# Gate and value projections by seven products of half-size blocks in place of eight, with the products sent to the down projection through DRAM

## The chip, the cores and the metric

One core of a Trainium2 chip (trn2). The metric is the device time of one execution in microseconds. The kernel before takes 2325.32 us, the median of 3 runs (2323.78 to 2327.04).

## The reference, cut to what matters

One layer of a hybrid model on 1024 prompt tokens and 8 x 4 sample tokens: a projection, a gated linear recurrence and sparse attention, an output projection, and then a feed-forward block with a short convolution over time. Only that last block is touched:

```python
def conv_ffn(h, conv_past, w_gate, w_val, conv_w, conv_b, w_down):
    u = h @ w_gate
    u_ext = jnp.concatenate([conv_past.astype(u.dtype), u], axis=1)
    c = conv_b + u_ext[:, 0:T] * conv_w[0]
    for j in range(1, CONV_W):
        c = c + u_ext[:, j:j + T] * conv_w[j]
    y = (jax.nn.gelu(c) * (h @ w_val)) @ w_down
    return y, u_ext[:, T:]
```

h is [1056, 1024] (prompt and samples together), w_gate and w_val are [1024, 2816], w_down is [2816, 1024], all float32. The last two rows of u of every sequence are outputs too.

## The kernel before, in words

Every large product is made with split operands: a value x is kept as a high part H (x rounded to fp32r by ScalarE) and a low part L = x - H (by VectorE), and a product is HH + HL + LH, three matmuls. The sizes: P = 128, TOK = 1056 tokens, KD = 8 blocks of 128 along the model axis, NF = 22 tiles of 128 along the feed-forward axis, PW = 352 = TOK / 3.

`project_out` (line 951) makes x1 = x + o @ w_out by tiles of 128 tokens (9 tiles, the last has 32) and the normalized, transposed h. For each tile VectorE adds (L1135), ScalarE squares (L1068), VectorE scales (L1101), TensorE transposes (L1170), and `keep_hT` (L1103) writes the high part of h (L1107) and, in four operations, the low part (L1111) for each of two halves of the model axis. They stay in SBUF for the next stage, as hH and hL. SyncE loads the first weights of the next stage at L1017.

`feed_forward` (line 1206) has two parts.

Projections. For each tile f of 128 features, first the gate (a = 0), then the value (a = 1): three parts of 352 tokens, 8 blocks along the model axis, 3 matmuls each, in the loop around L1585, which runs over f in hardware (Fori). Each tile's weights are [128, 8, 128]: SyncE loads them (L1299), ScalarE makes the high part (L1354), VectorE the low part (L1457). The gate's result is copied by ScalarE to U (L1361 to L1364), convolved over time by VectorE into C (L1470 to L1475, prompt and samples apart), put through gelu by ScalarE (L1369), and multiplied by VectorE with the value's result straight out of PSUM (L1490) into aT, which stays in SBUF, three tensors of [128, 22, 352] for the three parts of the tokens. GpSimd has nothing to do in this part.

Down projection. 12 units (3 parts of tokens x 4 quarters of the output), each of 11 pieces of w_down ([128, 2, 256], 256 KB; SyncE L1307, a ring of 4), each piece 12 matmuls (L1619). ScalarE and VectorE split each piece (L1379, L1497) and each pair of tiles of aT (L1390, L1502). Between them TensorE turns the results of the unit before (L1594), ScalarE copies (L1396), VectorE adds x1 (L1511) and normalizes at the end of each part (L1531). GpSimd issues the loads of x1 and the stores of y (L1324, L1330).

The order of the work on every engine is the order in which it is written; semaphores join the engines:

```python
            for i in range(2, PIECES):
                n, g = i // NGR, i % NGR
                high_w(i)
```

Of the kernel before, what the change touches and what calls it, by code (L numbers as in the profile page):

```python
# [5 lines left out]
F32 = mybir.dt.float32  # L6
# [944 lines left out]
def project_out(nc, io, keep, scratch, consts_sb):  # L951

    ident, hH, hL = consts_sb["ident"], keep["hH"], keep["hL"]
    with ExitStack() as ctx:
# [8 lines left out]
        oH, oL = keep["wH"], keep["wL"]  # L963
        sq = sb("sq", [P, D])
# [12 lines left out]
        hH_ready, low_added = sem("hH_ready"), sem("low_added")  # L977
        scaled = sem("scaled")
        rs = keep["hg_ss"]
# [17 lines left out]
        def _(sp):  # L997
# [18 lines left out]
            for a, w in enumerate(("w_gate", "w_val")):  # L1016
                sp.dma_start(keep["raw"][:, a], io[w][0].rearrange("(k p) n -> p k n", p=P)[:, :, 0:P]).then_inc(soft[f"p6_wu_in{a}"], 16)  # L1017
# [22 lines left out]
        def _(act):  # L1040
# [20 lines left out]
            for t in range(NT):  # L1061
# [6 lines left out]
                nc.scalar.activation(sq[0:r, :], x1[0:r, t % 2, :], ACT.Square, accum_out=ss[0:r, t:t + 1]).then_inc(ss_ready, 1)  # L1068
                act.wait_ge(ms_ready, t + 1)
                nc.scalar.activation(rt[0:r, t:t + 1], ss[0:r, t:t + 1], ACT.Sqrt).then_inc(root_ready, 1)  # L1070
                if t == 3:
                    act.wait_ge(conv_turned, 1)
                    turned = to[1][:].rearrange("p k c -> p (k c)")
                    nc.scalar.copy(keep["cw"][:].rearrange("p f j -> p (f j)"), turned[:, 0:20 * NF]).then_inc(conv_kept, 1)

        @block.vector
        def _(dve):
# [25 lines left out]
            def keep_hT(t):  # L1103
                r = rows_of(t)
                for h in range(2):
                    dve.wait_ge(hT_ready, 2 * t + h + 1)
                    nc.vector.tensor_tensor(hH[:, 4 * h:4 * h + 4, t * P:t * P + r], th[h][:, :, 0:r],  # L1107
                                            g2[:, 4 * h:4 * h + 4].unsqueeze(2).to_broadcast([P, 4, r]), ALU.mult).then_inc(hH_ready, 1)
                    dve.wait_ge(hH_ready, 2 * t + h + 1)
                    for k in range(4):  # L1110
                        last = nc.vector.scalar_tensor_tensor(hL[:, 4 * h + k, t * P:t * P + r], th[h][:, k, 0:r],  # L1111
                                                              g2[:, 4 * h + k:4 * h + k + 1],
                                                              hH[:, 4 * h + k, t * P:t * P + r].bitcast(F32), ALU.mult, ALU.subtract)
                    last.then_inc(hT_kept, 1)

            lows = Steps(dve, low_added)
# [5 lines left out]
            for t in range(NT):  # L1122
# [15 lines left out]
                if t >= 1:  # L1138
                    keep_hT(t - 1)
            keep_hT(NT - 1)  # L1140
# [64 lines left out]

def feed_forward(nc, io, keep, scratch, consts_sb):

    ident, small_tail = consts_sb["ident"], keep["tail_tok"]
# [1929 lines left out]
```

## Time and profile before

| | before |
|---|---|
| median of 3 runs | 2325.32 us (2323.78 to 2327.04) |
| the profiled execution | 2322.47 us, its span 2320.7 us |
| granted TensorE clock over the span | 0.966 |
| first matmul of the projections (L1585) | at 1537.28 us of the span |
| first matmul of the down projection (L1619) | at 2043.22 us |
| matmuls L1585 / L1619 | 3168 / 1584 |

Times in the profile are from the start of the span. PE is TensorE's matmuls, PEld its weight loads, DVE VectorE, ACT ScalarE, POOL GpSimd, SP SyncE; a q behind an engine's name is its queue. A matmul's own duration overlaps its neighbours': the distance between starts is what it costs.

### The profile page before, as it was taken

How to read it: one execution, taken by the hardware profiler on the slowest of the kernel's cores; microseconds unless marked ns; L12 is line 12 of the kernel's file. 1: busy time of each engine (PE TensorE's matmuls, PEld its weight loads, DVE VectorE, ACT ScalarE, POOL GpSimd, SP SyncE). 2: the span in 40 equal slices, each digit the busy share in tenths (PEclk: the TensorE clock that was granted, in tenths of full speed). 3: DMA queues.
4: the chain of work that ended last, by engine and by line, in shares of the span. 5: the costliest groups of instructions: out<-in, count | busy, mean ns of one | idle time of the engine just before them, and what ended most of it. 6: DMA issues, size and time to landing. Idle time of an engine off the chain costs nothing. (4 is left out here: it accounts for less than half of the span.)

```text
span 2320.7 us, 39113 instructions
## 1 busy us (share of the span) xinstructions
PE 2185.6 (94%) x15270; PEld 1973.0 (85%) x15270; DVE 1274.7 (55%) x2993; ACT 944.7 (41%) x2031; POOL 489.2 (21%) x835
## 2 busy tenths in 40 slices
PE   6999999999999999967798898989999999999998
PEld 5999997777777877745777786879999999999997
DVE  5123227776776777765687786543333333355543
ACT  4115114554554555534475674112222222245543
POOL 0001104333342333210386791100000000000000
PEclk9999999999999999978799999989999999999999
DMA  4216636655555555369010112311111111144553
GB/s 124 73 37 197 243 151 205 210 169 182 166 185 166 169 183 176 84 180 338 25 43 8 46 44 81 123 39 50 47 45 48 45 45 45 45 147 155 183 157 102
DMA packets 226386, 276.41 MB, mean 119 GB/s; under 512 B 24114, under 2 KB 195346, under 8 KB 216850
## 3 DMA queue, kind: packets, MB, share of 16 engines
q1 hardware_dynamic: 208568, 172.36, 24.5%
q0 software_dynamic: 17664, 101.98, 12.6%
q8 instruction: 98, 1.61, 0.3%
q14 instruction: 56, 0.46, 0.1%
HBM read 219.37 MB, written 61.81 MB: 121 GB/s over the span
## 5 line engine op out<-in xcount | busy, mean ns | idle before, releaser
L1585 PE MATMUL f<-hH,wH 128*128 128x352 f32 x1056 | 342.1, 324 | 4.0 <-DVE wL L1457 4.0
L1585 PE MATMUL f<-hL,wH 128*128 128x352 f32 x1056 | 339.8, 322 | 0.0
L1585 PE MATMUL f<-hH,wL 128*128 128x352 f32 x1056 | 339.3, 321 | 0.0
L2593 ACT CAST a_XTH<-cpt 64x256 fp32r<-64x256 f32 (+1 forms) x576 | 200.4, 348 | 144.8 <-PE cpt L2809 134.1
L2710 DVE TENSOR_TENSOR a_XTL<-cpt,a_XTH 64x256 fp32r<-64x256 f32 (+1 forms) x576 | 230.1, 399 | 28.8 <-ACT a_XTH L2593 20.4
L2824 PE MATMUL cph<-a_XTH,w1H 128*128 128x512 f32 x512 | 217.3, 424 | 0.0
L2824 PE MATMUL cph<-a_XTH,w1L 128*128 128x512 f32 x512 | 205.1, 401 | 0.0
L2824 PE MATMUL cph<-a_XTL,w1H 128*128 128x512 f32 x512 | 205.1, 401 | 0.0
L1585 PEld LDWEIGHTS f<-hH,wH 128*128 128x128 f32 x1056 | 199.2, 189 | 4.2 <-DVE wL L1457 4.2
L1585 PEld LDWEIGHTS f<-hL,wH 128*128 128x128 f32 x1056 | 199.4, 189 | 0.0
L1585 PEld LDWEIGHTS f<-hH,wL 128*128 128x128 f32 x1056 | 198.8, 188 | 0.0
L1457 DVE TENSOR_TENSOR wL<-raw,wH 128x1024 fp32r<-128x1024 f32 x44 | 53.8, 1225 | 225.5 <-ACT wH L1354 223.1
L1619 PE MATMUL f<-a_a_low,wH 128*128 128x352 f32 x528 | 171.6, 325 | 0.0
L1497 DVE TENSOR_TENSOR wL<-raw,wH 128x512 fp32r<-128x512 f32 x132 | 91.3, 692 | 126.9 <-ACT wH L1379 126.4
L1619 PE MATMUL f<-a_high,wH 128*128 128x352 f32 x432 | 139.9, 324 | 0.0
L1619 PE MATMUL f<-a_high,wL 128*128 128x352 f32 x432 | 139.5, 323 | 0.0
L1379 ACT CAST wH<-raw 128x512 fp32r<-128x512 f32 x132 | 81.4, 618 | 133.4 <-PE f L1619 120.9
L492 PE MATMUL pj<-wH,xL 128*128 128x256 f32 (+2 forms) x464 | 131.1, 282 | 0.0
L492 PE MATMUL pj<-wH,xH 128*128 128x256 f32 (+2 forms) x464 | 131.0, 282 | 0.0
L492 PE MATMUL pj<-wL,xH 128*128 128x256 f32 (+2 forms) x464 | 130.7, 282 | 0.0
L1354 ACT CAST wH<-raw 128x1024 fp32r<-128x1024 f32 x44 | 46.1, 1050 | 182.9 <-PE f L1585 175.9
L2824 PEld LDWEIGHTS cph<-a_XTL,w1H 128*128 128x128 f32 x512 | 98.2, 192 | 23.6
(506 smaller groups left out, 5330.0 us busy)
## 6 DMA issues: line engine op xcount, KB each, us to landing
raw<-in_w_down SPq DMA_DIRECT2D x132, 256.0 KB, 2.7
raw<-in_w_in POOLq DMA_DIRECT2D x12, 1024.0 KB, 6.0
a_V<-v_s SPq DMA_DIRECT2D x6, 2048.0 KB, 14.2
v_s<-X SPq DMA_DIRECT2D x22, 512.0 KB, 6.2
raw<-in_w_gate SPq DMA_DIRECT2D x22, 512.0 KB, 3.8
raw<-in_w_val SPq DMA_DIRECT2D x22, 512.0 KB, 3.8
z_tok<-stage SPq DMA_DIRECT2D x48, 128.0 KB, 4.7
a_akq<-hq SPq DMA_DIRECT2D x32, 192.0 KB, 5.4
```

The source lines that it names most:

```text
L492: last = nc.tensor.matmul(bank[u % 8][0:r, 0:nw], xp[:, k, a * P:a * P + r], wp[:, j % 2, k, 0:nw], **flags)
L1354: nc.scalar.copy(wH[:, a].rearrange("p k n -> p (k n)"), raw[:, a].rearrange("p k n -> p (k n)")).then_inc(wH_ready, 1)
L1379: nc.scalar.copy(slot(wH, i), slot(raw, i)).then_inc(wdH_ready, 1)
L1457: nc.vector.tensor_tensor(wL[:, a], raw[:, a], wH[:, a].bitcast(F32), ALU.subtract).then_inc(wL_ready, 1)
L1497: nc.vector.tensor_tensor(slot(wL, i), slot(raw, i), slot(wH, i).bitcast(F32), ALU.subtract).then_inc(wdL_ready, 1)
L1585: last = nc.tensor.matmul(bank[3 * a + n][:, 0:w], wp[:, a, k, :], hp[:, k, c0:c0 + w], start=(k + part == 0), stop=(k == KD - 1 and part ...
L1619: last = nc.tensor.matmul(acc(n, o), slot(w, i)[:, j, P * o:P * o + P], a, start=(f + part == 0), stop=(f == NF - 1 and part == 2))
L2593: nc.scalar.copy(turned(XTH, u, s, k, g, a), split(bank(at, k)[:], u, k, g, a)).then_inc(h_ready, 1)
L2710: last = nc.vector.tensor_tensor(turned(XTL, u, s, k, g, a), split(bank(at, k)[:], u, k, g, a), hi.bitcast(F32), ALU.subtract)
L2824: last = nc.tensor.matmul(out[:, :, 0:n], w[:, s, k, q, m * P:(m + 1) * P], x[:, s % 2, k, :, q:q + n], **flags)
```

## The change

Each block of 256 features (two tiles) of w_gate or w_val is cut in 2 x 2 blocks (W00, W01, W10, W11: half of the model axis, tile of features), and h, for each half c of the tokens (528), in 2 x 2 blocks too (half of the model axis, 264 tokens left or right). The product of 2 x 2 blocks is made with seven block products (M1 to M7) of sums and differences. q counts 22 blocks: even q is the gate of tiles q and q+1, odd q the value of the tiles of q-1. A product is 4 x 3 = 12 matmuls of 264 columns; M1, M6, M7, M4 gather in one PSUM bank, M5 and M3 in another, M2 in a third, and ScalarE copies the partial sums after M1, M6 and M7 to mt. The sums of the weights are GpSimd's, in float32, before the split; those of h VectorE's.

The gated product is formed in three places (GpSimd for M2, M5, M3 of the value, VectorE for M4), in C, and no longer stays in SBUF: each tile goes to a DRAM tensor a_T and comes back for the down projection, the first part in 11 loads by SyncE, the other two in one load each by GpSimd.

`project_out` keeps one float32 copy of h (hf) instead of two parts, and makes five of the 14 block pairs of h; the squares go to xs instead of a tensor of their own. The loops over features are unrolled. Weight splits run seven weights ahead (a ring of 7 in place of 2 buffers). The head's order differs, and the last block's is half by half.

The order of the products, and the rest that the prediction speaks of:

```diff
+    order = [(0, r, c) for c in range(2) for r in (M1, M2, M6, M5, M7, M4)]
+    for q in range(1, LAST):
+        for x in [(q, M1), (q - 1, M3)] + [(q, r) for r in (M6, M2, M7, M5, M4)]:
+            order += [x + (0,), x + (1,)]
+    order += [(LAST - 1, M3, 0), (LAST - 1, M3, 1)]
+    order += [(LAST, r, c) for c in range(2) for r in (M1, M6, M2, M7, M5, M4, M3)]
...
+    head = {None: [("w", 0), ("w", 1), ("b", 0, M3)], (0, M1, 0): [("b", 0, M4), ("w", 2)], (0, M2, 0): [("w", 3), ("w", 4), ("b", 1, M1)],
+            (0, M6, 0): [("w", 5), ("b", 1, M2)], (0, M5, 0): [("b", 1, M5)], (0, M7, 0): [("b", 1, M6)], (0, M4, 0): [("b", 1, M7)],
+            (0, M1, 1): [("b", 1, M4)], (0, M2, 1): [("b", 1, M3)], (0, M6, 1): [("w", 6), ("w", 7)], (0, M5, 1): [("w", 8)],
+            (0, M7, 1): [("w", 9), ("w", 10)], (0, M4, 1): [("w", 11), ("w", 12)]}
+    def ahead(x):
+        if x is None or x[0] == 0 and x in head:
+            return head[x]
+        n = index[x[0], x[1]] + SLOTS
+        return [("w", n)] if x[2] == 1 and n < len(mats) else []
...
         @block.sync
+            def raw_in(q):
+                if q == 1:
+                    sp.wait_ge(bL_ready, max(b_at[0, M3], b_at[0, M4]))
+                else:
+                    sp.wait_ge(L_ready, all_split(q - 2))
+                i = q // 2
+                sp.dma_start(raw[q % 2][:], w_up[q % 2][:, :, 2 * P * i:2 * P * i + 2 * P]).then_inc(wu_in[q % 2], 16)
+            def pair_out(i, j, c=None):
+                q = 2 * i + 1
+                e = 1 if c is None else c
+                sp.wait_ge(multiplied, multiplied_at[q, M5 if j else M3, e])
+                if j:
+                    sp.wait_ge(added, added_at[q, M4, e])
+                at = slice(0, TOK) if c is None else slice(2 * HW * c, 2 * HW * c + 2 * HW)
+                sp.dma_start(scratch["a_T"][2 * i + j][:, at], C[j][:, at]).then_inc(a_out, 16)
+            raw_in(1)
+            for q in range(1, LAST):
+                raw_in(q + 1) if q + 1 <= LAST else None
+                if q % 2 == 0:
+                    pair_out(q // 2 - 1, 0)
+                else:
+                    pair_out(q // 2, 1)
+            for i in range(RING):
+                piece_in(i)
+            sp.wait_ge(product, done_at[LAST, M7, 0])
+            sp.wait_ge(a_out, 16 * 2 * (NGR - 1))
+            for j in range(NGR - 1):
+                front_in(j)
+            for c in range(2):
+                for j in (1, 0):
+                    pair_out(NGR - 1, j, c)
+                if c == 0:
+                    sp.wait_ge(a_out, 16 * 2 * NGR)
+                    front_in(NGR - 1)
+            for i in range(RING, PIECES):
+                piece_in(i)
...
         @block.gpsimd
+            def weight_sums(q):
+                a = lambda r: part_of_w(q, r)
+                if q >= 1:
+                    pool.wait_ge(wu_in[q % 2], 16 * (q // 2 + 1))
+                    pool.wait_ge(L_ready, index[q - 1, M5] + 1)
+                    pool.wait_ge(L_ready, index[q - 1, M6] + 1)
+                    pool.wait_ge(s_ready, s_at[q - 1, M3])
...
+                nc.gpsimd.tensor_tensor(S[:, 0], a(M7), a(M4), ALU.add).then_inc(s_ready, 1)
+                pool.wait_ge(s_ready, s_at[q, M5])
+                nc.gpsimd.tensor_tensor(S[:, 1], S[:, 0], a(M1), ALU.subtract).then_inc(s_ready, 1)
+                pool.wait_ge(s_ready, s_at[q, M6])
+                nc.gpsimd.tensor_tensor(a(M7), a(M1), a(M7), ALU.subtract).then_inc(s_ready, 1)
...
+            for q in range(1, LAST):
+                weight_sums(q + 1)
+                if q >= 2 and not gate(q - 1):
+                    for c in range(2):
+                        times_gate(q - 1, M3, c)
+                if not gate(q):
+                    for c in range(2):
+                        times_gate(q, M2, c)
+                fourth_sum(q + 1)
+                if not gate(q):
+                    for c in range(2):
+                        times_gate(q, M5, c)
...
         @block.scalar
+            def keep_product(q, r, c):
+                act.wait_ge(product, done_at[q, r, c])
...
+                m, before = {M1: (0, M2), M6: (1, M3), M7: (2, M5)}[r]
+                if q >= 1:
+                    if gate(q - 1):
+                        act.wait_ge(added, added_at[q - 1, before, c])
+                    else:
+                        act.wait_ge(multiplied, multiplied_at[q - 1, before, c])
+                nc.scalar.copy(mt[:, m, c], out_bank(q, r, c)).then_inc(kept, 1)
...
+            for x in order:
+                q, r, c = x
+                if x in kept_at:
+                    keep_product(*x)
+                split(ahead(x))
+                if q >= 1 and not gate(q):
+                    if (r, c) == ((M1, 1) if q < LAST else (M1, 0)):
+                        gelu(q // 2, 1)
+                    if (r, c) == ((M2, 1) if q < LAST else (M7, 0)):
+                        gelu(q // 2, 0)
...
         @block.vector
+            for x in order:
+                q, r, c = x
+                if x in added_at:
+                    combine(*x)
+                split(ahead(x))
+                if gate(q) and (r, c) == (M4, 1):
+                    conv(q // 2, 1)
+                if gate(q) and (r, c) == (M3, 1):
+                    conv(q // 2, 0)
...
         @block.tensor
+            def one_product(q, r, c):
+                n = index[q, r]
+                pe.wait_ge(L_ready, n + 1)
+                if q == 0 and (c, r) in b_at:
+                    pe.wait_ge(bL_ready, b_at[c, r])
...
+                if r in (M6, M7, M4):
+                    pe.wait_ge(kept, kept_at[q, {M6: M1, M7: M6, M4: M7}[r], c])
+                if r == M3:
+                    pe.wait_ge(added, added_at[q, M5, c])
...
+                for k in range(4):
+                    for part, (w, x) in enumerate(((WH(n), BH(c, r)), (WH(n), BL(c, r)), (WL(n), BH(c, r)))):
+                        last = nc.tensor.matmul(out_bank(q, r, c), w[:, k], x[:, k], start=begins and k + part == 0,
+                                                stop=k == 3 and part == 2, skip_group_check=True)
+                last.then_inc(product, 1)
```

## Rows read from the trace of the kernel before

**Rows 1.** The page: busy time, and 40 slices (tenths).

```profile
PE 2185.6 (94%) x15270; PEld 1973.0 (85%) x15270; DVE 1274.7 (55%) x2993; ACT 944.7 (41%) x2031; POOL 489.2 (21%) x835
...
PEclk9999999999999999978799999989999999999999
DMA  4216636655555555369010112311111111144553
```

**Rows 2.** The chain that ended last, in order of time: start us, us, what.

```profile
1537.28 505.95 PE f L1585 x3168
2043.22 23.23 PE f L1619 x144
...
2093.43 21.30 PE f L1619 x132
```

**Rows 3.** Timeline of PE, two stretches of L492: start us, us, engine line op.

```profile
239.75 0.28 PE L492 MATMUL pj<-wH,xH 128*128 128x256 f32 x1
...
242.59 0.28 PE L492 MATMUL pj<-wH,xH 128*128 128x256 f32 x1
...
338.10 0.29 PE L492 MATMUL pj<-wH,xH 128*128 128x280 f32 x1
...
341.18 0.29 PE L492 MATMUL pj<-wH,xH 128*128 128x280 f32 x1
```

**Rows 4.** Timeline of DVE at the end of project_out.

```profile
1516.84 0.69 DVE L1135 TENSOR_TENSOR a_x<-py,a_x 128x512 f32<-128x512 f32 x1 [4.81 <-PE py L1196]
...
1520.75 1.13 DVE L1111 SCALAR_TENSOR_TENSOR hL<-th,a_g,hH 128x128 fp32r<-128x128 f32 x4
...
1534.82 0.09 DVE L1448 MEMSET a_U<- 128x2 f32 x2 [0.35 <-PEq L954]
```

**Rows 5.** Groups of ACT and DVE by form: count, busy us, mean ns, idle before.

```profile
L1379 ACT CAST wH<-raw 128x512 fp32r<-128x512 f32 x132 | 81.4, 618 | 133.4 <-PE f L1619 120.9 <-DMA raw<-in_w_down 7.8 <-PE f L1585 4.7
L1361 ACT COPY a_U<-f 128x352 f32<-128x352 f32 x22 | 9.9, 448 | 8.4 <-PE f L1585 8.4
...
L1497 DVE TENSOR_TENSOR wL<-raw,wH 128x512 fp32r<-128x512 f32 x132 | 91.3, 692 | 126.9 <-ACT wH L1379 126.4
L1457 DVE TENSOR_TENSOR wL<-raw,wH 128x1024 fp32r<-128x1024 f32 x44 | 53.8, 1225 | 225.5 <-ACT wH L1354 223.1
L1472 DVE SCALAR_TENSOR_TENSOR a_C<-a_U,a_cwj,a_C 128x1024 f32<-128x1024 f32 x22 | 28.3, 1285 | 0.8
L1470 DVE TENSOR_SCALAR a_C<-a_U,a_cwj 128x1024 f32<-128x1024 f32 x22 | 17.9, 812 | 8.2 <-ACT a_U L1364 7.5
L1511 DVE TENSOR_TENSOR y_rows<-y_rows,f 128x256 f32<-128x256 f32 x16 | 6.0, 415 | 8.2 <-PE f L1594 8.2
L1473 DVE SCALAR_TENSOR_TENSOR a_C<-a_U,a_cwj,a_C 128x32 f32<-128x32 f32 x22 | 5.5, 252 | 0.8
```

**Rows 6.** Groups of POOL: a form's mean ns (128 wide), a line's min/median/max ns (512).

```profile
L2366 POOL TENSOR_TENSOR a_ob<-a_ob,a_gin 128x128 f32<-128x128 f32 x32 | 14.8, 461 | 2.5
L1025 POOL TENSOR_TENSOR a_o<-a_o,hg_ss x7: 1029/1059/1473, 1417.8 to 1495.1; 128x512 f32<-128x512 f32 x6, 32x512 f32<-32x512 f32 x1
```

**Rows 7.** DMA issues: tensors, queue, count, KB each, median us to landing.

```profile
raw<-in_w_in POOLq DMA_DIRECT2D x12, 1024.0 KB, 6.0
raw<-in_w_gate SPq DMA_DIRECT2D x22, 512.0 KB, 3.8
w<-in_cmp_w POOLq DMA_DIRECT2D x4, 1024.0 KB, 10.1
out_y_prompt<-y_rows SPq DMA_DIRECT2D x2, 512.0 KB, 2.7
```

**Rows 8.** Timelines of DVE and POOL, from 1409 to 1421 us.

```profile
1411.40 2.05 DVE L1080 TENSOR_TENSOR wL<-w5a,wH 128x1024 fp32r<-128x1024 f32 x1 [3.39 <-ACT wH L1043]
...
1410.34 2.04 POOL L1025 TENSOR_TENSOR o_front<-o_front,hg_ss 128x512 f32<-128x512 f32 x2 [14.37 <-POOLq L565]
```

**Rows 9.** Busy us of each engine in a stretch, PEclk, DMA share, GB/s.

```profile
2043.00:2060.00 17.00, 17.00 (x107) 17.00 (x106) 14.33 (x21) 11.16 (x18) 2.12 (x4) 1.00 0.75 238
```

More of the change, by code:

```diff
@@ new lines, in feed_forward @@
+        b0c = sb("b0c", [P, 2, 2, 4, HW], F32R)
+        b1 = sb("b1", [P, 7, 2, 4, HW], F32R)
+        ring = keep["ring"] + [sb(f"ring{i}", [P, 2, 4, P], F32R) for i in range(4, SLOTS)]
+        S = sb("S", [P, 2, 4, P])
+        mt = sb("mt", [P, 3, 2, HW])
+        raw = [keep["raw"], keep["raw1"]]
+        quarter = keep["quarter"]
+        bset = dict(keep["b"])
+        bset.update({(0, M4): b0c[:, 0], (0, M3): b0c[:, 1]})
+        bset.update({(1, m): b1[:, m] for m in range(7)})
+        BH, BL = (lambda c, m: bset[c, m][:, 0]), (lambda c, m: bset[c, m][:, 1])
@@ L1459, in product_tile @@
[L1459 to L1469 removed]
+            b, step = Steps(dve, b_step), Steps(dve, c_step)
@@ new lines, in split, with combine @@
+            def split(items):
+                for what, *x in items:
+                    (low_of_w if what == "w" else low_of_b)(*x)
+            def combine(q, r, c):
+                dve.wait_ge(product, done_at[q, r, c])
+                z = out_bank(q, r, c)
+                if r == M4:
+                    dve.wait_ge(g_ready, 2 * (q // 2) + 1)
+                    nc.vector.tensor_tensor(C[1][:, left(c)], z, C[1][:, left(c)], ALU.mult).then_inc(added, 1)
+                    return
+                m, of, j, at = {M2: (0, M1, 0, left(c)), M5: (2, M7, 1, right(c)), M3: (1, M6, 0, right(c))}[r]
+                dve.wait_ge(kept, kept_at[q, of, c])
+                if not gate(q):
+                    nc.vector.tensor_tensor(mt[:, m, c], z, mt[:, m, c], ALU.add).then_inc(added, 1)
+                    return
+                if q == 0:
+                    dve.wait_ge(bL_ready, max(b_at[0, M3], b_at[0, M4]))
+                n = min(HW, T - at.start)
+                last = nc.vector.tensor_tensor(U[j][:, 2 + at.start:2 + at.start + n], z[:, 0:n], mt[:, m, c, 0:n], ALU.add)
+                if n < HW:
+                    rows = lambda v: v[:, n:HW].rearrange("p (b t) -> p b t", b=DB)
+                    last = nc.vector.tensor_tensor(sample(U[j], 2), rows(z), rows(mt[:, m, c]), ALU.add)
+                last.then_inc(added, 1)
@@ L1604, in turn_tails @@
                 last.then_inc(t_ready, 1)
+            for x in order:
+                one_product(*x)
             for i in range(PIECES):
```

463 lines of the change are left out of this document (277 added, 186 removed).

## The prediction

> **What bounds the kernel now.** I read the page first. TensorE is busy 94% of the span and its clock is full in the whole second half, while the DMA engines are at a tenth of their time in slices 27 to 35 [rows 1]. The chain that ended last puts a name on it: one unbroken piece of 505.95 us holds the 3168 matmuls of the gate and value projections, and the down projection follows at once in pieces of 132 matmuls in about 21.3 us [rows 2]. So this stage is TensorE's own pace, and an edit pays only by what it takes from that pace and gives back in waits. The reader should take the spacing from the chain (505.95 / 3168 = 0.1597 us), not from the 0.32 us that a matmul row shows, since matmuls overlap.
>
> **The matmuls.** Before: 44 tiles of 128 features x 3 parts x 8 x 3 = 3168 matmuls of 352 columns. After: 22 blocks of 256 features x 2 halves of the tokens x 7 products x 4 x 3 = 3696 matmuls of 264 columns. That is 17% more instructions, so the question is what one costs. No row has 264 columns, but two are near: 25 matmuls of 256 columns start 2.84 us from first to last, 0.1183 each, and 25 of 280 columns 3.08 us, 0.1283 [rows 3]. Between them 264 gives 0.1217; the line from 256 to 352 gives 0.1218. The bounds are those two rows: 437 and 474 us for 3696. A product is 12 matmuls, 1.46 us. Groups of 12 cost a little more than long ones (21.30 / 132 = 0.1614 against 0.1597 [rows 2], some 0.02 a group), so I take **1.47 us a product**: 308 x 1.47 = 452.8 us against 505.95, a gross gain of 53.
>
> **The end of the attention output's stage.** Per tile of 128 tokens the four low-part operations of each half go (1.13 us twice, [rows 4]) and only the scaled copy stays. Added after tile 6 are four operations of VectorE over 1056 elements, and four more later, at 1225 x 1056 / 1024 = 1.26 us each [rows 5]. After tile 6 VectorE had to wait 4.81 us for TensorE before its next x1 half, so that is covered. After tile 7, 3 x 1.26 come in and 2.3 go before the x1 of tile 8; behind it 1.26 come in and 3.7 go. Of this net 1 us I count 0.3, since the transposes between have waits of their own: the new stage starts at 1534.5 instead of 1534.8 [rows 4]. The raw weights now come in one load of 1 MB, long before.
>
> **The head (block 0).** Here nothing is ahead. TensorE needs for each product a weight pair and, for the first time, a pair of activation blocks. VectorE makes the low parts in the order written: 0.69 us for a weight, 1.26 for an activation block, and 1.26 for each difference of blocks [rows 5]. In us from 1534.5: weight 0 is ready at 1.4, and there TensorE starts (1.3 earlier than before, since the first split is half as long); the difference and the split for (0, M4) push the weight of M6 to 8.0, where TensorE has waited since 4.3; combine, two weights and the first block of half 1 with two differences run to 13.6; the weight of M4 comes at 14.3, block M2 of half 1 at 15.6, M6 at 20.9, M7 at 22.1, M4 at 25.7. TensorE ends M4 of half 1 at about 28. Of this 12 x 1.47 = 17.6 are work, so **some 9 us of gaps**. Its bounds: 17.6 if every gap closes, 31 if four of VectorE's operations collide with GpSimd's first sums as in [rows 8]. VectorE leaves the head with a backlog (low parts, then a convolution of 4.7 us), but the ring of seven weights covers it.
>
> **The steady blocks.** Per pair of blocks, TensorE needs 28 x 1.47 = 41.2 us. VectorE: 14 weight splits 9.7, 14 combines at 0.43 and the four short sample parts 7.0, two convolutions with their small copies (0.81 + 2 x 1.285 + short ones) 9.6: 26 us. ScalarE: 14 x 0.62 + 14 copies of 264 columns at about 0.37 (0.448 for 352) + 2 gelus at 1.2 by the same slope: 16 us. GpSimd, new here: 8 sums of 512 at 1.06 and 6 products of 264, between 0.46 and 1.06, say 0.69 [rows 6]: 12.6 us. None is the bound by its sum. The order within a pair is what counts.
>
> I followed who waits for whom. In each even block q from 2 to 20, the copy of M6's partial sum (ScalarE) needs the buffer that GpSimd frees by multiplying (q-1, M3). In GpSimd's order three weight sums of block q+1 stand before that multiplication, and they need that block's raw weights. SyncE asks for these only after the store of the pair's second tile, which waits for the last combine of block q-1. From the start of block q: the last product's results 0.16, combine 0.42 [rows 5], the store's issue 0.4: request at 1.0. The load is 1 MB; the nearest row, of the same size and row length, lands in 6.0 [rows 7]. The store of 528 KB stands ahead of it in the queue; the nearest row, 512 KB by SyncE, needs 2.7 in all, of which I count 1.1. Landed at 8.1. Three sums 3.3: 11.4. The multiplication 0.7: 12.1. The copy 0.42: 12.5. M7 of block q is due after 8 products, at 11.8. So TensorE stands **0.8 us** in each even block even if nothing collides. M7 of the other half is due 1.47 later and its buffer comes 0.7 later, so it adds nothing.
>
> It will collide: a VectorE subtraction of 1024 elements that takes 1.22 alone took 2.05 while GpSimd multiplied [rows 8]. In the same stretch VectorE splits two weights. Between 0 and two such delays (2 x 0.83) are possible; I take 0.9, and 0.2 for the odd blocks, where the convolution, the gelu behind it and the copy of M7 come within half a us of their due times. That makes 1.9 a pair, **19 us** for ten pairs. With a landing of 3.8 (the row of 512 KB) it is 0; with 10.1 (the slower 1 MB row of [rows 7]) it is 4.9 + 1.7 = 6.6, or 66 us.
>
> **The last block and the seam.** In block 21 M6 follows M1 of the same half directly and waits for its copy: 2 x 0.6. The down projection's first pieces lie ready. The front of the activations comes back in ten loads of 352 KB; by the slope from 512 KB to 1 MB ([rows 7], 1.1 us per 256 KB) a pair lands each 1.5 us, and TensorE eats one in 12 x 0.161 = 1.94, with 15 us of head start. Piece 4 of w_down is now queued behind the last stores, which wait for GpSimd: asked for at 2.5 us after the last product, split at 7, due at 7.8. In the 17 us after the seam the DMA engines were busy 0.75 already [rows 9], and 4 MB more of activations come on GpSimd's queue. I take 1 us; bounds 0 and 6 (three late pieces). The reload for the third part falls into unit 4, when copies are not due for 50 us: nothing.
>
> **The sum.** Start 1534.5 + head 28.1 + 296 x 1.47 = 435.1 + 1.2 makes 1998.9, against the seam at 2043.2 [rows 2]: 44.3 us earlier before stalls. Less 19 for the even and odd blocks and 1 for the seam: 24.3. The profiled execution took 2322.5, so 2298 in its terms; the median of the runs shown is 2.9 above it, and on it I get **2301**.
>
> **The rivals.** (1) No stall: the raw load lands within 7.3 us of the block's start, that is, takes under 5.2 itself. For it: w_gate's loads of 512 KB land in 3.8. Gain 43, time 2282. (2) Slower: the raw load of the odd blocks. Its place is the chain SyncE, GpSimd, ScalarE above; its price is one for one beyond a landing of 7.3; it decides when the stall passes 4.9 a pair (44.3 - 49 = -4.7), that is a load of over 9 us of its own, behind its store and with one collision. For it: the 10.1 of w<-in_cmp_w; at 6.6 a pair the time is 2348. Against it: the queue is empty here, where that row had other traffic. (3) VectorE and GpSimd exclude each other. By [rows 8] they did once; if all 12.6 us of GpSimd stood in VectorE's way, a pair would need 38.6 of 41.2, still under TensorE, but the convolution would end at 8.5 instead of 5.2 in an odd block (three sums of 1.1 in its way), the gelu and the copies with it, and M7 and M4 would wait 1 to 3 us a pair: 10 x 2 more than my sum, 2321. (4) The edit does not do what it says: spacing does not follow the columns. At 0.16 a matmul, 3696 would take 591 and the kernel be slower by 85; [rows 3] speak against it outright.
>
> The Trainium skill ("SBUF — State Buffer", Who interferes with whom) says that a VectorE operation with two SBUF inputs and a GpSimd operation that reads SBUF exclude each other for a whole instruction. That is rival (3), and the trace agrees where it shows the pair, with 2.05 for 1.22.
>
> **Chances.** Forecast 0.50; (1) 0.22; (3) 0.14, half of it still faster; (2) 0.09; (4) 0.01; seam or head beyond their bounds 0.04. What a measurement here can tell from no change is 0.2%, 4.7 us: faster needs under 2320.7. Faster 0.83, same 0.07, slower 0.10. The range takes in (1) and most of (3): 2279 to 2322; it leaves out (2) and (4).
>
> **What would show it.** Right: 264-column matmuls at 0.122 apart; a first product at about 1536; gaps of 9 us in the head, ended by VectorE's low parts; in each even block one idle of TensorE before (q, M7, 0), ended by ScalarE's copy of M6, behind it GpSimd's product and the landing of raw. Wrong: idle before another product, a spacing off by over 0.003 (11 us), or a load that lands over 9 us after its issue.

## The result, and the profile after

The changed kernel takes 2339.94 us (median of 10 runs, 2332.12 to 2346.15), the kernel before beside it 2327.41 (10 runs): ratio 1.0055, 95% interval 1.0041 to 1.0069. It is slower by 12.5 us; 2301 was forecast, with 24 us gained.

The page first, to hold against [rows 1].

```profile
PE 2156.6 (92%) x15798; PEld 1936.6 (83%) x15798; DVE 1404.7 (60%) x3143; ACT 1005.2 (43%) x2202; POOL 681.6 (29%) x991
...
PEclk9999999999999999978799999989999999999999
DMA  4216646655554555459100112311221221475643
...
PE 23%; DMA 4%; DVE 3%; issue 2%; POOL 2%; ACT 1%; DVEq 0%; ACTq 0%; POOLq 0%; SPq 0%
PE f L1824 12%; PE f L1865 10%; DMA raw_odd<-in_w_val 3%; DMA raw<-in_w_down 2%; POOL a_S L1468 1%; POOL a_S L1466 1%; DVE a_ring L1664 0%; DVE C L1722 0%; PE f L1834 0%; POOL C L1481 0%; ACT a_mt L1571 0%; ACT a_ring L1545 0%; DVE C L1720 0%; DVE hf L1667 0%; DVE ring L1664 0%
```

TensorE is busy 29 us less, and the kernel is slower all the same: time that matmuls took has become waiting. The last two lines, the chain that ended last by engine and by line, say where (the share of a line is of the whole span). Of before it was one piece of matmuls over the whole stage [rows 2]; now it passes through two loads (raw_odd, the value weights, and raw, the pieces of w_down) and GpSimd's sums (L1466, L1468). L1824 are the projections' matmuls, L1865 the down projection's.

Reading the starts of the matmuls of each stage gives the balance of the two profiled executions (before 2322.47 us, after 2340.44):

| | before | after | forecast |
|---|---|---|---|
| first matmul of the projections | 1537.28 | 1541.63 | 1536 |
| projections, from it to the first of the down projection | 505.8 | 502.75 | 482 |
| down projection, first to last matmul | 264.95 | 281.1 | 266 |

The first line says nothing of the change. Its matmul comes between 1530.1 and 1542.0 in the executions below, whose code ahead of it is the same. The other two lines, -3.0 and +16.1, sum to 13.1, near the 12.5 us between the medians.

**Inside the projections.** A product starts 1.46 us after the one before wherever nothing waits, as forecast (1.47). "Idle" before a product is, from here on, the distance of its start from the start before it, less 1.46. The rest is in the chain of waits. This is its part in block 8 (start us, us, what), a block like every other even one:

```profile
1724.97 7.42 PE f L1824 x61
1732.39 0.02 issue
1732.41 0.63 ACT a_ring L1545
1733.04 0.02 issue
1733.07 0.66 DVE a_ring L1664
1733.72 6.26 DMA raw_odd<-in_w_val
1739.98 0.07 issue
1740.05 1.30 POOL a_S L1466
1741.35 0.07 issue
1741.42 1.63 POOL a_S L1468
...
1743.30 1.39 issue
1744.69 0.74 POOL C L1481
...
1745.51 0.39 ACT a_mt L1571
1745.90 0.14 issue
1746.03 14.09 PE f L1824 x114
```

This is the forecast chain link by link: SyncE asks late, the load lands, three sums of GpSimd (the third lies in the "issue" of 1.39), its multiplication, ScalarE's copy of M6, and only then M7. The block started at 1732.2. Request at +1.5 (forecast +1.0), landed +7.8 (+8.1), sums done +12.5 (+11.4), multiplied +13.2 (+12.1), M7 at +13.8, due at +11.7. The idle before M7 is 2.1 us here and 1.7 to 3.4 in all ten even blocks, 23.9 in sum.

Behind it comes a cost that was not in the sum. Two views of block 6, TensorE's timeline and then two stretches (columns: stretch, its us, busy us of PE, PEld, DVE, ACT and POOL, the granted clock, DMA share, GB/s):

```profile
1696.67 1.63 PE L1824 MATMUL f<-a_b,ring 128*128 128x264 f32 x12
1701.45 2.98 PE L1824 MATMUL f<-b0a,ring 128*128 128x264 f32 x12 [3.16 <-ACT a_mt L1571]
1704.23 1.90 PE L1824 MATMUL f<-a_b,ring 128*128 128x264 f32 x12
1705.97 1.62 PE L1824 MATMUL f<-b0b,a_ring 128*128 128x264 f32 x12
```

```profile
1701.00:1704.00 3.00, 2.55 (x11) 2.58 (x12) 1.44 (x4) 1.73 (x4) 0.54 (x1) 0.57 0.57 179
1704.00:1708.00 4.00, 4.00 (x31) 4.00 (x31) 1.43 (x3) 1.28 (x3) 1.29 (x1) 0.90 0.80 265
```

The product behind the idle of 3.3 us (3.16 by the profile's own reading) takes 2.78 us to the start of the next one, instead of 1.46: the granted clock stands at 0.57 there, near its lower level of 1.2 GHz (0.5), and averages 0.90 over the next 4 us. By their starts, the three products behind each idle cost 9.6 us more than 1.46 each, over the ten even blocks, and slow products cost another 5.5 in the head. Not every idle brings it: blocks 8 and 10 stand idle 2.14 and 2.09 us; behind the first no product takes more than 1.53, behind the second one takes 2.64.

The odd blocks lose 2.3 us in all (before M7 and M4 of block 1, none later), the last block 2.3.

**The seam.** Counting 132 matmuls to a unit, start to start, the down projection's unit 0 takes 31.2 us (before 21.3), unit 4 26.4 and unit 5 23.3 (together 49.7; before 43.9), the others as before. The chain there:

```profile
2047.15 0.61 DVE wdL L1729
2047.76 0.01 SPq L1417
2047.77 0.04 issue
2047.81 10.19 DMA raw<-in_w_down
...
2058.08 0.63 ACT wdH L1583
...
2058.73 0.70 DVE wdL L1729
...
2059.45 12.60 DMA raw<-in_w_down
```

A piece of 256 KB lands in 2.8 us in the median of the whole stage; here the two on the chain, the seventh and the eleventh, take 10.2 and 12.6. The fifth is not the trouble: asked for 2.4 us into the unit, it lands in 4.5, and TensorE waits 0.5 us for it. The seven behind it take 8 to 13. The next fences give the DMA line (40 slices of 1 us) and the transfers asked for, from 2040 to 2080, after and then before, and the two kernels' own busy rows of unit 0:

```profile
DMA  8210479898999999999999999999999950299856
...
a_aT<-a_T POOLq DMA_DIRECT2D x1, 3872.0 KB, 19.2
raw<-in_w_down SPq DMA_DIRECT2D x15, 256.0 KB, 6.6
...
2044.40:2075.60 31.20, 23.15 (x135) 21.10 (x134) 16.05 (x22) 10.33 (x17) 4.80 (x6) 1.00 0.93 312
```

```profile
DMA  9100369999999995535748471618170530521606
...
raw<-in_w_down SPq DMA_DIRECT2D x18, 256.0 KB, 3.3
y_rows<-x POOLq DMA_DIRECT2D x2, 512.0 KB, 4.3
...
2043.00:2064.30 21.30, 21.30 (x134) 21.30 (x133) 15.81 (x23) 12.40 (x20) 2.12 (x4) 1.00 0.72 228
```

The DMA engines are full for 25 us and move 312 GB/s in place of 228. Before, SyncE asked for pieces from 2038.30 on without a break, ahead of the seam. Now it issues the last stores between, and the fifth piece is asked for at 2046.8, when TensorE is in the second of its four. The rows of x1 are no news (before asks for them at 2043.5, and they are the y_rows of its fence), nor are busy engines; the lead of the pieces is gone, and 3.9 MB are new. Then all come together: GpSimd's rows of x1 (1.4 MB, L1486, at 2046.99), its second part of the activations (3.9 MB, L1495, at 2050.96) and the pieces.

### The profile page after: what moved, and what is told of

It is laid out like the page before. It is cut to its first block and busy times, and to the rows that moved or that the text cites. A ratio compares the mean times of both kernels' runs of the same rounds, so it can differ in the third digit from the quotient of the medians.

```text
span 2338.5 us, 40872 instructions
## 1 busy us (share of the span) xinstructions
PE 2156.6 (92%) x15798; PEld 1936.6 (83%) x15798; DVE 1404.7 (60%) x3143; ACT 1005.2 (43%) x2202; POOL 681.6 (29%) x991
## 5 line engine op out<-in xcount | busy, mean ns | idle before, releaser
L2956 DVE TENSOR_TENSOR a_XTL<-cpt,a_XTH 64x256 fp32r<-64x256 f32 (+1 forms) x576 | 230.0, 399 | 32.1 <-ACT a_XTH L2839 23.7
L1865 PE MATMUL f<-a_aH,wdH 128*128 128x352 f32 x528 | 174.3, 330 | 11.3 <-DVE wdL L1729 11.3
L1865 PE MATMUL f<-a_aH,wdL 128*128 128x352 f32 x528 | 171.5, 325 | 0.0
L1824 PE MATMUL f<-a_b,ring 128*128 128x264 f32 x1056 | 148.9, 293 | 3.5 <-ACT a_mt L1571 3.5
L1824 PE MATMUL f<-b0a,ring 128*128 128x264 f32 x804 | 116.5, 298 | 31.1 <-ACT a_mt L1571 24.3
L1824 PEld LDWEIGHTS f<-a_b,ring 128*128 128x128 f32 x1056 | 140.6, 197 | 3.9 <-issue 3.9
L1824 PEld LDWEIGHTS f<-b0a,ring 128*128 128x128 f32 x804 | 108.5, 200 | 33.8 <-issue 26.5
L492 PE MATMUL pj<-wH,xL 128*128 128x256 f32 (+2 forms) x464 | 130.9, 282 | 0.0
L492 PE MATMUL pj<-wH,xH 128*128 128x256 f32 (+2 forms) x464 | 130.9, 282 | 0.0
L492 PE MATMUL pj<-wL,xH 128*128 128x256 f32 (+2 forms) x464 | 130.5, 281 | 0.0
L662 POOL TENSOR_SCALAR a_Prs<-a_Prs,a_cf 128x128 f32<-128x128 f32 (+7 forms) x64 | 110.1, 1737 | 22.5 <-DVE a_cf L807 22.4
L3070 PEld LDWEIGHTS cph<-a_XTH,w1H 128*128 128x128 f32 x512 | 98.5, 192 | 18.8
L1865 PE MATMUL f<-aL,wdH 128*128 128x352 f32 x352 | 113.6, 323 | 0.0
L3070 PEld LDWEIGHTS cph<-a_XTH,w1L 128*128 128x128 f32 x512 | 98.8, 193 | 17.8
```

Of the source, the lines that this page charges most:

```text
L492: last = nc.tensor.matmul(bank[u % 8][0:r, 0:nw], xp[:, k, a * P:a * P + r], wp[:, j % 2, k, 0:nw], **flags)
L662: nc.gpsimd.tensor_scalar(Pr_of(u)[:, h, 0:u.w], Pr_of(u)[:, h, 0:u.w], cf[:, u.n, h:h + 1], None, ALU.mult).then_inc(p_ready, 1)
L1824: last = nc.tensor.matmul(out_bank(q, r, c), w[:, k], x[:, k], start=begins and k + part == 0, stop=k == 3 and part == 2, skip_group_check ...
L1865: last = nc.tensor.matmul(acc(n, o), wd_slot(w, i)[:, j, P * o:P * o + P], a, start=(f + part == 0), stop=(f == NF - 1 and part == 2))
L2956: last = nc.vector.tensor_tensor(turned(XTL, u, s, k, g, a), split(bank(at, k)[:], u, k, g, a), hi.bitcast(F32), ALU.subtract)
L3070: last = nc.tensor.matmul(out[:, :, 0:n], w[:, s, k, q, m * P:(m + 1) * P], x[:, s % 2, k, :, q:q + n], **flags)
```

## The experiments

Theory at the start: the loss has two places of about equal size, the late request for the raw weights in the projections, and bursts on the DMA engines at the seam and at the third part's reload. Rivals: GpSimd itself is too slow or sits in VectorE's way (projections); the place in SyncE's queue, not the load of the engines, delays the pieces (seam). Times are medians of 4 to 10 executions; "idle" is TensorE's before M7 of the even blocks, in sum.

| run | time, us | ratio to before (interval) | projections | idle | unit 0 | unit 1 | units 4+5 | down projection |
|---|---|---|---|---|---|---|---|---|
| before | 2327.41 | 1 | 505.8 | - | 21.3 | 24.4 | 43.9 | 264.95 |
| after | 2339.94 | 1.0055 (1.0041 to 1.0069) | 502.75 | 23.9 | 31.2 | 24.3 | 49.7 | 281.1 |
| raw_early | 2298.48 | 0.9877 (0.9860 to 0.9893) | 468.9 | 0 | 32.3 | 24.3 | 48.9 | 281.3 |
| pool_order | 2305.24 | 0.9913 (0.9897 to 0.9930) | 477.2 | 6.1 | 31.3 | 24.3 | 48.6 | 280.0 |
| no_diffs | 2296.82 | 0.9874 (0.9845 to 0.9903) | 466.3 | 0 | 30.9 | 24.4 | 48.7 | 279.8 |
| w2_first | 2305.35 | 0.9910 (0.9882 to 0.9939) | 470.7 | 0 | 32.1 | 24.3 | 48.5 | 280.6 |
| part_late | 2332.38 | 1.0024 (1.0007 to 1.0041) | 506.2 | 25.1 | 28.0 | 24.3 | 49.4 | 277.5 |
| wd_first | 2334.89 | 1.0041 (1.0024 to 1.0058) | 503.4 | 24.2 | 29.9 | 24.4 | 48.5 | 278.6 |
| paced | 2329.60 | 1.0015 (0.9998 to 1.0032) | 502.7 | 23.9 | 27.9 | 24.3 | 44.3 | 272.1 |
| rows_late | 2329.58 | 1.0034 (1.0019 to 1.0049) | 503.6 | 24.0 | 21.4 | 28.2 | 48.5 | 273.8 |
| wd_rows | 2328.48 | 1.0023 (1.0005 to 1.0041) | 502.0 | 24.4 | 21.3 | 26.8 | 48.6 | 272.3 |
| early_paced | 2292.93 | 0.9880 (0.9857 to 0.9904) | 470.4 | 0 | 27.9 | 24.3 | 44.3 | 272.1 |
| best | 2291.49 | 0.9852 (0.9826 to 0.9877) | 470.5 | 0 | 21.3 | 24.3 | 44.3 | 265.5 |

The kernel before, run beside each, had medians from 2323.0 to 2327.4, so ratios are what to compare. The columns from the fourth on are of the one profiled execution. How far those scatter can be read from unit 0 in the five kernels whose seam has the same code (after, raw_early, pool_order, no_diffs, w2_first): 30.9 to 32.3.

### raw_early: the request a block earlier

```diff
-                raw_in(q + 1) if q + 1 <= LAST else None
-                if q % 2 == 0:
-                    pair_out(q // 2 - 1, 0)
-                else:
+                if q % 2 == 1:
+                    raw_in(q + 1)
+                    if q + 2 <= LAST:
+                        raw_in(q + 2)
                     pair_out(q // 2, 1)
+                else:
+                    pair_out(q // 2 - 1, 0)
```

The semaphore a_out is split in two, one for each tile of a pair, so that the stores may be in another order; nothing is computed otherwise.

> One edit: SyncE asks for an odd block's raw weights before the store that waits for the last combine (the counts of the two tiles' stores are kept apart for it). Theory A (the late raw block is the whole cause of the even blocks' stalls): the ten idles before M7 of an even block (24.0 us together) go under 1 us, the matmuls at the low clock behind them (some 8 us) go too, the kernel takes about 2308 us. Rival B (GpSimd's sums are too slow by themselves, 4.65 us for three while VectorE works beside them): idles of 1 us or more stay, about 2325. Rival C (the projections give the time back elsewhere: DMA or the ring of weights): the gap moves to another product, above 2330.

Theory A holds, and the time is 10 us under the 2308 expected. SyncE asks for the raw weights of block 9 10.3 us before block 8 starts, where it was 1.5 after. All ten idles are gone, and with them the slow products behind them; the projections take 468.9 us. The chain holds one piece from block 1 to the seam, and the stretch below has the full clock:

```profile
1586.69 391.31 PE f L1827 x3216
```

```profile
1570.00:2000.00 430.00, 426.43 (x3499) 425.52 (x3498) 282.85 (x512) 156.72 (x312) 175.71 (x144) 1.00 0.26 85
```

391.31 / 3216 = 0.1217 us a matmul of 264 columns, the forecast's own figure. The changed kernel's stretch has 0.98 for the clock and 407.06 for PE. GpSimd does all the sums still (175.7 us busy) and the chain no longer passes through it: only the time of its start was wrong. The projections give back 33.8 us: the 23.9 of idle and the 9.6 of slow products behind it make 33.5.

### pool_order: the multiplication ahead of the sums

```diff
-                weight_sums(q + 1)
                 if q >= 2 and not gate(q - 1):
                     for c in range(2):
                         times_gate(q - 1, M3, c)
+                weight_sums(q + 1)
```

> One edit: GpSimd multiplies (q-1, M3) before it sums the weights of block q+1; the raw load stays as late as it is. Theory A1 (the stall goes through GpSimd's order: multiplication behind sums behind the load): the idles before M7 go under 1 us although raw still lands 7.9 us into the block; about 2308. Rival A2 (the stall goes through ScalarE, which waits for the same load for the high part of its first weight and has the copy of M6 behind it): ScalarE is free at 8.5 us, M7 is due at 11.7, so this rival says that nothing is left as well unless ScalarE then waits for a sum: idles before M7 or M5 of 1 us or more, 2320 or above.

The load is as late as in the change, yet the idle falls to 6.1 us (most of it in blocks 6, 14 and 16, with 2.3, 1.6 and 0.5) and the projections to 477.2. So for 17.8 of the 23.9 us it was not the weights that M7 lacked but the buffer behind GpSimd's queue: the multiplication had its data and stood behind sums that had none. The 6.1 that stay were not expected by theory A1 (all idles under 1 us). They have another ender: TensorE's idle in the whole stage is now put down to VectorE's weight low parts, 24.8 us in 17 waits, head included and matmuls and their weight loads both counted (columns: releaser, us, times); in raw_early the same line has 14.0 in 4. In block 6 ScalarE stands 7.3 us for the late load itself, with the split of M7's weight behind it, and TensorE waits for that weight's low part; so the rest goes by rival A2's way, at a smaller price than it named.

```profile
  DVE ring L1664: 24.8, 17
  issue: 8.8, 8
```

### The head: no_diffs and w2_first

Both stand on raw_early. no_diffs makes the five differences of blocks of h in the head on one column only; the products that use them are so not the reference's.

```diff
-            less = lambda out, x, y: b(nc.vector.tensor_tensor(out, x, y, ALU.subtract))
+            less = lambda out, x, y: b(nc.vector.tensor_tensor(ss[:, 0:1, 0:1], x[:, 0:1, 0:1], y[:, 0:1, 0:1], ALU.subtract))
```

> On the kernel with the early raw load: five differences of blocks of h in the head (1.26 us each on VectorE) are left out, a one-column operation stands in their place; the output isn't the reference's. Theory H (the head is VectorE's sum of work): block 0 ends 5 to 6 us earlier, 2293. Rival (the head is bound by TensorE at the low clock, or by ScalarE): under 2 us, 2297.

The head ends 29.75 us after its first product, against 31.9: 2.2 us, between the 5 to 6 of theory H and the rival's "under 2"; the medians do not tell the kernel from raw_early (ratios 0.9874 and 0.9877). VectorE's five operations took 8.4 us in raw_early (three of 1.25, two of 2.33) and take 2.9 here, so of 5.5 us less work only 2.2 were on the path. VectorE waits for ScalarE's high part 1.21 us at three of its low parts in both kernels; here it also waits 0.71, 0.21 and 0.89 us, for ScalarE too, where it did not before. Two of the one-column operations last 1.2 us, the other three 0.15. Those two run beside a sum of GpSimd's and end with it (VectorE's rows, then GpSimd's):

```profile
1550.89 1.24 DVE L1670 TENSOR_TENSOR a_ss<-hf 128x1 f32<-128x1 f32 x1
1553.34 2.44 DVE L1676 TENSOR_TENSOR a_b<-hf,a_b 128x1056 fp32r<-128x1056 f32 x2 [1.21 <-ACT a_b L1553]
1555.69 0.15 DVE L1670 TENSOR_TENSOR a_ss<-hf 128x1 f32<-128x1 f32 x1
...
1549.93 2.18 POOL L1473 TENSOR_TENSOR raw_odd<-raw_odd 128x512 f32<-128x512 f32 x1
```

w2_first puts M6's weight ahead of M4's blocks:

```diff
-    head = {None: [("w", 0), ("w", 1), ("b", 0, M3)], (0, M1, 0): [("b", 0, M4), ("w", 2)],
+    head = {None: [("w", 0), ("w", 1), ("b", 0, M3)], (0, M1, 0): [("w", 2), ("b", 0, M4)],
```

> On the kernel with the early raw load: in the head, the weight of M6 is split before the blocks for M4 instead of behind them. Theory H (VectorE's sum, not its order): the gap of 3.9 us before M6 goes, and the same time comes back before a product of the second half; the kernel gains under 1 us, 2298. Rival (order): it gains 3 us or more, 2295.

M6 comes without its gap, and the time turns up later: M5 waits 3.0 us, M4 0.9, M6 of the second half 3.8, M4 0.7, 8.97 in all with what is shorter, where it was 8.96 in the change and in raw_early. The order only moves the gap. The head as a whole is longer, 33.9 us, by more products at the low clock, and the projections by 1.7. The median is 6.9 us above raw_early's, which neither expectation has; of the 5.9 us between the two profiled executions 5.0 lie ahead of the projections, where the code is the same. So only that the order gains nothing is shown.

### The seam: which transfer starves the pieces

part_late asks for the second part of the activations (3.9 MB) only when unit 0 is done; wd_first asks for the fifth and sixth piece ahead of the last two stores; rows_late asks for the first rows of x1 (1.4 MB) after eight pieces, and, since the load of the second part stands behind the rows in GpSimd's queue, for that part too. What is said of each rests on the units of the profiled execution; the intervals of the ratios overlap or touch.

```diff
+            pool.wait_ge(d_ready, 1)
             part_in(1)
```

```diff
             for c in range(2):
+                if c == 1:
+                    for i in range(RING, RING + 2):
+                        piece_in(i)
                 for j in (1, 0):
                     pair_out(NGR - 1, j, c)
...
-            for i in range(RING, PIECES):
+            for i in range(RING + 2, PIECES):
                 piece_in(i)
```

```diff
             pool.wait_ge(multiplied, len(pool_order))
+            pool.wait_ge(w_used, 8)
             rows_in(0)
```

> One edit: the 3.9 MB load of the second part of the activations waits for the end of unit 0. Theory D (one burst of 3.9 MB starves the 256 KB pieces of w_down wherever it falls): unit 0 falls from 31.2 to 21.5 us, unit 1 or 2 grows by about 6 (as unit 4 and 5 did together, 5.9): 3 to 5 us less, about 2336. Rival E (unit 0 is late because pieces 4 and on are queued behind the last stores, which wait for GpSimd): unit 0 stays at 29 us or more and the time at 2340.

Unit 0 is 28.0, 3.2 us less and not all of 10: just under rival E's 29 or more, and far from theory D's 21.5. The load now falls into unit 1, which takes 24.3, before the change 24.4: the same 3.9 MB there, without the rows beside them, cost nothing.

> One edit on the changed kernel: SyncE asks for pieces 4 and 5 of w_down before the last two stores of the activations, not behind them. Theory E (queue place): both land before the seam's rush, the 4 us step before piece 5 goes and unit 0 falls from 31.2 to 26 us or less; 2 to 5 us less than the changed kernel. Rival D (the DMA engines are full with 1.4 MB of x1 and 3.9 MB of activations, and pieces 6 to 10 wait all the same): unit 0 stays at 30 or more.

Unit 0 is 29.9, 1.3 us less, against a scatter of 30.9 to 32.3: close to rival D's 30, and a small gain if any. The fifth to seventh pieces come in time, and TensorE now waits for the eighth, the ninth, the eleventh and unit 1's first. The order in SyncE's queue decides which pieces are late, and has little to do with how late they are.

> The changed kernel with one wait added: GpSimd asks for the first x1 rows of the last stage (1.4 MB) only after eight pieces of w_down are used, not at once behind its last product. Three bursts meet at the seam (last stores, the second part of the activations of 3.9 MB, these rows); moving the second and third parts to paced loads took 3.3 us from unit 0, moving the stores 1.3, and with the rows late as well unit 0 was as before the change, 21.3. Theory R (the rows are what starves the pieces): unit 0 of the down projection falls from 31.2 to under 25, since the 3.9 MB part alone fits between the pieces; units 4 and 5 stay at 26.4 and 23.3; time of the changed kernel less 6 to 8, so 2332 to 2334. Theory B (any 4 MB burst on the shared DMA engines does it, whichever is there): unit 0 stays at 28 to 30, time less 1 to 3.

Unit 0 is 21.4. But this is not theory R's case, for the 3.9 MB moved with the rows. GpSimd's timeline has both loads late, 16 to 18 us into the unit:

```profile
2056.54 1.65 POOL L1486 DMA_DIRECT2D y_rows<-x  x3 [14.36 <-PE f L1866]
2058.18 1.39 POOL L1495 DMA_DIRECT2D a_aT<-a_T  x1
```

What unit 0 pays is so: 27.9 to 28.0 with the rows alone beside the last stores (part_late, paced, early_paced), 30.9 to 32.3 with rows and part, 21.3 to 21.4 with neither. The part without the rows was not run at the seam. The rows alone cost nothing in the kernel before, which asks for them at the same place with the pieces running ahead. Unit 1 takes 28.2 in place of 24.3, since rows and part now come together there; the chain has two loads of pieces:

```profile
2056.43 5.32 DMA raw<-in_w_down
...
2063.20 15.20 DMA raw<-in_w_down
```

So of 9.8 us gained 3.9 come back in the next unit, with a full ring of pieces; the ratio, 1.0034, is 0.2% under the change's, and the intervals overlap.

> The changed kernel with pieces 4 and 5 of w_down asked for before the last stores, and the x1 rows asked for after eight pieces; the two parts of the activations still come in loads of 3.9 MB. Theory R: unit 0 at 21.3 to 23, time 2329 to 2332. Theory B: the 3.9 MB part still delays the pieces behind the fifth, unit 0 at 26 to 28, and the third part still costs units 4 and 5 some 5 us.

wd_rows is wd_first and rows_late in one. Unit 0 is 21.3, and unit 1 26.8, 1.4 less than in rows_late. The down projection is 8.8 us shorter than in the change, where rows_late alone gave 7.3 and wd_first 2.4; the third part's reload still costs units 4 and 5 almost what it did. Theory B's 26 to 28 for unit 0 is out, but again both of GpSimd's loads are late.

paced leaves GpSimd's two bulk loads out and has SyncE bring the second and third parts in 22 loads of 352 KB, one behind every second piece of w_down:

```diff
+            def pair_in(p, j):
+                if p == 2 and j == 0:
+                    sp.wait_ge(d_ready, NQ)
+                sp.dma_start(aT[p][:, 2 * j:2 * j + 2], scratch["a_T"][2 * j:2 * j + 2, :, PW * p:PW * p + PW].rearrange("f p t -> p f t")).then_inc(front_ready[j], 16)
...
                 piece_in(i)
+                for p, first in ((1, 8), (2, 50)):
+                    if first <= i <= first + 20 and (i - first) % 2 == 0:
+                        pair_in(p, (i - first) // 2)
```

> One edit: the second and third part of the activations come in 22 loads of 352 KB by SyncE, one behind every second piece of w_down, instead of two loads of 3.9 MB by GpSimd. Theory D (burst): units 0, 4 and 5 fall from 31.2, 26.4 and 23.3 us to about 22.5, 22 and 22: 14 to 15 us less, about 2325. Rival E (order of the queue): unit 0 stays at 29 or more, only units 4 and 5 gain: about 2334.

Units 4 and 5 are at 22.1 and 22.2, as theory D has it: of the 5.9 us that the third part cost there 0.4 are left. Unit 0 is at 27.9, which neither theory has (22.5, or 29 and more), as in part_late: the rows are still in its way.

### Together: early_paced and best

early_paced is raw_early with paced; best is these two with wd_first and rows_late.

> Raw weights asked for a block early (as in raw_early, 2298.5) and the second and third parts of the activations in loads of 352 KB paced by the pieces (as in paced); stores and rows as in the change. If the costs of projections and seam add, the time is that of raw_early less 3.3 in unit 0 and 5.4 in units 4 and 5: 2290 to 2292 before the noise of one execution in the stages ahead. If relief at one place is given back at the other (the stall had spaced the transfers), it stays at 2296 or more. Theory R: unit 0 near 28; theory B: under 25.

> All edits together: raw weights of odd blocks asked for before the store, activations back in 22 paced loads by SyncE, pieces 4 and 5 of w_down before the last stores, x1 of the first part only after 8 pieces. Theory: 2298.5 of the first edit alone, less 6.5 (units 4 and 5) and less 6 to 9 (unit 0 at 22 us): 2284 to 2287. If the seam is starved by something else (the ten front loads), unit 0 stays at 27 and the time is near 2291.

In the profiled executions the gains of the two places add: early_paced has nearly raw_early's projections (470.4 for 468.9) and paced's units 0, 4 and 5 (27.9, 22.1 and 22.2). The times show less: its median is 5.5 us under raw_early's, but the two ran beside kernels before of 2323.3 and 2325.8, and the ratios are the same, 0.9880 and 0.9877. In best unit 0 is 21.3; its down projection takes 265.5 us where the kernel before took 264.95, and its projections 470.5 for 505.8. Its median, 2291.5, is over the 2284 to 2287 expected, though the profiled execution took 2286.8. best is faster than the kernel before by 1.5% and than the change by 2%. Its busy row of the seam shows that full DMA engines are not in themselves the trouble:

```profile
2007.00:2030.00 23.00, 23.00 (x146) 22.87 (x145) 15.82 (x21) 11.42 (x19) 3.41 (x5) 1.00 0.93 297
```

0.93 of the engines' time and 297 GB/s, almost as in the change (0.93, 312), and TensorE never waits. What differs is that the second part comes in small loads between the pieces, that the rows come later, and the lead that the pieces have. This run does not take the three apart.

The medians of best and early_paced are 1.4 us apart and their intervals overlap, though the profiles differ by 6.6 in the down projection; the stages ahead vary by as much between executions, so the medians do not tell these two apart.

## Why the prediction was wrong

- **Product and spacing: right.** 1.46 us for 1.47, and 0.1217 us a matmul over 3216 in a row. Rival (4) is out.
- **The mechanism of the stall: right**, with request, landing, sums, multiplication and copy in this order; raw_early takes it away by its first link, pool_order most of it by its fourth.
- **Its size: the first term that failed.** "Three sums 3.3" took 4.65. They were costed at the 1.06 of [rows 6]; GpSimd's sum of 512 elements takes 1.29, its operands cut from a wider tile, and 1.60 to 1.63 where VectorE splits a weight beside it. With the request 0.5 later and the landing 0.8 shorter that makes 2.1 in this block where 0.8 + 0.9 was allowed, 23.9 in all for 17.
- **The clock: a term that was missing.** The forecast took a stall to cost what it lasts. Slow products behind it cost 9.6 us more, and 5.5 in the head. So the even blocks cost 33.5 against 17: 16.5 of the 20.8 us that the projections are over the forecast.
- **Head, odd and last blocks.** The head's gaps are 8.96 us, with 9 forecast; 7.1 of them, before M6 of both halves, are ended by VectorE's low parts as written, the two of 0.7 before M4 by ScalarE's copy of M7. The head ends 31.9 us after its first product, with 26.7 forecast (28.1 less the 1.4 to the first product) and 31 as the head's upper bound; the difference is the low clock. Odd blocks 2.3 for 2, the last block 2.3 for 1.2; the spacing gave 3 back.
- **The seam: the step that failed most.** "I take 1 us; bounds 0 and 6" was some 10, and "the reload for the third part falls into unit 4 ...: nothing" was 6. What the working says of the fifth piece came true (asked for 2.4 us into the unit; forecast 2.5 us after the last product and no wait, measured a wait of 0.5). It named the 4 MB on GpSimd's queue and gave them no price of their own: it looked only at when each transfer is needed by its own reader. The third part is indeed not needed for 50 us; it is the pieces beside it that are. The prediction had [rows 9] in hand, 0.75 of the engines busy, and did not ask what rows and part together would do to a ring of four pieces that TensorE empties in 8 us.
- **The rivals.** (1), no stall, did not come; raw_early shows what it is worth, a ratio of 0.9877 even with the seam's loss. (2) did not come either: the load landed in 6.2 us, as forecast, not in over 9, and the stall came to 2.4 a pair, 3.4 with the clock, short of the 4.9 from which it decides. (3) is true in its mechanism and not in its place. In block 8 VectorE's split of a weight takes 1.18 in place of 0.69 beside GpSimd's sums, and these 1.6 in place of 1.29. That GpSimd and VectorE exclude each other (the Trainium skill, "SBUF — State Buffer", Who interferes with whom) fits these rows: the instruction that starts second is late by what is left of the first, less some 0.15 us (the split starts with 0.63 us of the first sum left and is 0.49 late; the second sum with 0.47 left is 0.34 late), and in no_diffs a subtraction of one column lasts 1.24 us, up to the end of GpSimd's sum. But the odd blocks, where the rival puts its loss, lose nothing after the first, and with the load early the same collisions cost TensorE nothing. "Seam or head beyond their bounds", given a chance of 0.04, is what came, of both.

The sum put right, in the forecast's terms: 2301 + 21 for the projections + 15 for the seam = 2337, against 2339.94.

Left open: why the same idle of 2.1 us brings a slow product in one block and not in the next; the time lost ahead of the projections in single executions; what the 3.9 MB would cost at the seam without the rows, and what the rows would cost with the fifth and sixth pieces ahead of them; and whether the head could be shortened by giving ScalarE and VectorE equal shares, which was not tried.

## What to carry over

A saving on the engine that bounds is only as good as the lead of what feeds it: follow each buffer to the queue entry that frees it, and put a request whose data are ready to be asked for, or an operation whose inputs are there, ahead of those that wait. A bulk load with a distant due time is not free: it is paid by the short loads that share the DMA engines, so cost it, together with every other load asked for at the time, at the ring with the least lead. Send it in pieces between the short loads; waiting until the ring has filled was enough for 3.9 MB alone (part_late, unit 1), not for 3.9 and 1.4 MB together (rows_late, unit 1). A stall of two or three microseconds on TensorE can cost half as much again through the clock. And an edit that holds back one request holds back all that stand behind it in the queue: look where each of them went before reading the result.

## What was not expected of the hardware

- A 256 KB load that lands in 2.8 us in the median took 8 to 13 us beside 3.9 MB and 1.4 MB of GpSimd's queue, with the DMA engines full at 300 to 400 GB/s for most of that time, and up to 10 beside either alone (part_late, units 0 and 1). The 3.9 MB alone, beside a ring that was full, cost TensorE nothing.
- TensorE's granted clock fell to 0.57 in the stretch read behind an idle of 3.3 us. Behind six of the ten idles in even blocks (2.0 to 3.4 us; the other four were 1.7 to 2.1) a product took 2.5 to 2.8 us in place of 1.46, behind the other four none took over 1.6.
- GpSimd's sum of 512 elements took 1.29 us with operands cut out of a wider tile, against 1.03 to 1.06 in [rows 6], and its product of 264 elements 0.74 to 0.76 alone.
- A VectorE subtraction of one column took 1.24 us beside a GpSimd sum and 0.15 alone.
